# Transposes of the identity issued in TensorE's pauses at the four normalisations of a two-layer decoder trunk

## The reference

```
h = x
# layer 0
hn = rmsnorm(h, attn_norm[0]); h = h + hgrn2_mixer(hn, ...)      # gated recurrence, 8 heads, chunks of 64
hn = rmsnorm(h, ffn_norm[0]);  h = h + (silu(hn @ w_gate) * (hn @ w_up)) @ w_down     # 2816 hidden
k_band, v_band = shared_kv(h, kv_norm, kv_w, k_gain)             # its own rmsnorm of the same h
# layer 1
hn = rmsnorm(h, attn_norm[1]); h = h + swa_attention(hn, k_band, v_band, ...)
hn = rmsnorm(h, ffn_norm[1]);  h = h + moe_swiglu(hn, ...)       # top 2 of 8 experts, 3584 hidden
```

## Time and profile before

| What | Value |
|---|---|
| device time, three runs | 1426.94, 1434.97 and 1435.8 us, median 1434.97 |
| the profiled execution: device time | 1431.02 us |
| the profiled execution: span | 1428.3 us, so 2.7 us lie around it |
| mean granted TensorE clock | 0.977 of full speed |
| TensorE matmul busy | 1349.9 us, 95% of the span |
| VectorE, ScalarE, GpSimd busy | 334.2, 256.8 and 21.1 us |
| DMA | 442.49 MB, mean 310 GB/s |

### The profile page before, as it was taken

How to read it: one execution, slowest core, us unless ns; L and a number is a source line. 1 busy time by engine, 2 the same in 40 slices (tenths; PEclk the granted TensorE clock), 3 DMA queues, 4 the chain that set the end, 5 groups by cost and what they waited for, 6 DMA issues and landing times.

```text
span 1428.3 us, 32690 instructions
## 1 busy us (share of the span) xinstructions
PE 1349.9 (95%) x14751; PEld 795.1 (56%) x14751; DVE 334.2 (23%) x449; ACT 256.8 (18%) x367; POOL 21.1 (1%) x27
## 2 busy tenths in 40 slices
PE   6998899998889799999999999999999999999994
PEld 5997799987657533533543443453453453353352
DVE  5664455453676400000000000000000000000001
ACT  5453444433533100000000000000000000000000
POOL 0001000000000100000000000000000000000001
PEclk9999899999899799999999999999999999999997
DMA  9972455555521698699999999999999999999994
GB/s 324 327 236 73 131 178 184 200 181 182 183 73 60 263 354 307 259 419 343 389 419 391 378 417 405 377 414 414 361 412 419 358 410 420 368 407 420 379 388 169
DMA packets 123540, 442.49 MB, mean 310 GB/s; under 512 B 9028, under 2 KB 50196, under 8 KB 107028
## 3 DMA queue, kind: packets, MB, share of 16 engines
q1 hardware_dynamic: 117844, 425.24, 78.8%
q10 hardware_dynamic: 4416, 11.04, 2.1%
q0 software_dynamic: 1152, 4.19, 0.8%
HBM read 434.12 MB, written 12.08 MB: 312 GB/s over the span
## 4 chain that ended last, share of the span: by engine, by line
PE 93%; DVE 3%; DMA 1%; ACT 1%; issue 1%; POOL 0%; SPq 0%; POOLq 0%; DVEq 0%; ACTq 0%
PE bank L1481 41%; PE bank L1496 21%; PE bank L1167 8%; PE bank L1168 8%; PE bank L1169 8%; PE bank L1526 1%; PE bank L1186 1%; PE bank L1539 1%; PE bank L1376 1%; PE bank L1471 1%; PE bank L1268 1%; PE bank L1463 1%; PE bank L1332 0%; DMA raw<-in_hgrn_w_in 0%; DVE w_lo L742 0%
## 5 line engine op out<-in xcount | busy, mean ns | idle before, releaser
L1481 PE MATMUL bank<-raw,xT 128*32 128x512 f32 (+1 forms) x4608 | 442.1, 541 | 4.0 <-issue 3.3
L1481 PEld LDWEIGHTS bank<-raw,xT 128*32 128x32 f32 x4608 | 150.8, 110 | 284.7 <-issue 284.7
L1496 PE MATMUL bank<-dn,hidT 128*32 128x256 f32 x5376 | 296.5, 379 | 0.0
L1496 PEld LDWEIGHTS bank<-dn,hidT 128*32 128x32 f32 x5376 | 172.3, 110 | 116.1 <-issue 4.4
L742 DVE TENSOR_TENSOR w_lo<-raw,w_hi 128x2048 fp32r<-128x2048 f32 x63 | 144.1, 2291 | 123.8 <-ACT w_hi L509 123.6
L1142 DVE TENSOR_TENSOR e_hid<-e_silu,bank 128x512 f32<-128x512 f32 (+1 forms) x48 | 26.9, 617 | 532.1 <-PE bank L1481 532.1
L1481 PE MATMUL bank<-up_more,xT 128*32 128x384 f32 (+1 forms) x1536 | 150.2, 539 | 0.0
L1167 PE MATMUL bank<-ht_hi,w_hi 128*128 128x256 f32 x480 | 136.2, 284 | 0.0
L1168 PE MATMUL bank<-ht_lo,w_hi 128*128 128x256 f32 x480 | 135.7, 283 | 0.0
L1169 PE MATMUL bank<-ht_hi,w_lo 128*128 128x256 f32 x480 | 135.6, 282 | 0.0
L509 ACT ACTIVATE w_hi<-raw 128x2048 fp32r<-128x2048 f32 x63 | 120.1, 1908 | 60.2 <-PE bank L1169 59.5
(11 more groups left out here) (232 smaller groups left out, 807.4 us busy)
## 6 DMA issues: line engine op xcount, KB each, us to landing
dn<-in_moe_w_down SPq DMA_DIRECT2D x112, 1024.0 KB, 12.5
raw<-in_moe_w_gate SPq DMA_DIRECT2D x48, 1024.0 KB, 13.5
raw<-in_moe_w_up SPq DMA_DIRECT2D x48, 1024.0 KB, 12.1
raw<-in_moe_w_gate SPq DMA_DIRECT2D x48, 768.0 KB, 9.2
raw<-in_moe_w_up SPq DMA_DIRECT2D x48, 768.0 KB, 6.3
raw<-in_hgrn_w_in SPq DMA_DIRECT2D x16, 1024.0 KB, 11.3
up_more<-in_moe_w_gate SPq DMA_DIRECT2D x16, 1024.0 KB, 21.7
up_more<-in_moe_w_up SPq DMA_DIRECT2D x16, 1024.0 KB, 12.3
```

What stands on the lines that cost most here:

```text
L1481: ins = nc.tensor.matmul(out_banks[j][GTOK * c:GTOK * c + GTOK, 0:w], xT[:, kt, GTOK * g:GTOK * g + GTOK], chunk[:, w * b:w * b + w], star ...
L1496: ins = nc.tensor.matmul(banks[6 + j // 2][GTOK * c:GTOK * c + GTOK, 256 * (j % 2):256 * (j % 2) + 256], tok, dn[:, i % DN_RING, D * half ...
```

## The change

A helper `keep_busy(n, bank)` issues n transposes of the 128 by 128 identity, with the identity also as the operand that does the turning, into a bank that nobody reads. It is called ahead of the first quarter of each normalisation, and at the first three also between the second and the third quarter. These transposes wait on no semaphore and signal none. The counts are 8 and 16 at the first normalisation, 32 and 14 at the second, 50 and 16 at the third, and 38 at the fourth: 174 in all.

```diff
+            def keep_busy(n, bank):
+
+                for i in range(n):
+                    nc.tensor.transpose(bank[:, P * (i % 4):P * (i % 4) + P], ident, ident)
+
-            def turn_norm(i):
-
+            def turn_norm(i, bank, before, between):
+
+                keep_busy(before, bank)
                 for u in range(4):
+                    if u == 2:
+                        keep_busy(between, bank)
                     pe.wait_ge(xs_ready, 2 * (i - 1) + 1 + u // 2)
                     turn_rows(lambda t: xs[:, t, :], [u])
@@
-            turn_norm(1)
+            turn_norm(1, banks[5], 8, 16)
@@
-            turn_norm(2)
+            turn_norm(2, banks[5], 32, 14)
@@
-            turn_norm(3)
+            turn_norm(3, banks[1], 50, 16)
@@
             since = tp[0]
+            keep_busy(38, banks[0])
             for u in range(4 + 1):
                 if u < 4:
                     pe.wait_ge(hn_ready, 1 + u // 2)
                     turn_rows(lambda t: xs[:, t, :], [u])
```

## The result

| | before | after |
|---|---|---|
| device time, median of 6 runs each | 1433.3 us (1425.64 to 1435.8) | 1421.38 us (1417.76 to 1422.35) |
| ratio, 95% interval | | 0.9925 (0.9895 to 0.9954) |
| span of the profiled execution | 1428.3 us | 1420.1 us |
| mean granted clock | 0.977 | 0.983 |

The change gained 0.75%, some 11 us (4 to 15 us by the interval). The runs of before differ by how long the clock was at half: at a mean granted clock of 0.974 to 0.975 they take some 1434 us, at 0.979 some 1426, and a median of a few moves between the two.

The account below looks back on a forecast made before the run. TensorE was taken to bound the kernel, busy 95% of the span, its expert block only moving. Gains of 5.8 us less 1.6 given back make 4.2, so 1430.8 us against the median 1434.97; range 1425 to 1438.

Parts of the forecast that it names:

- The clock part: Ahead of the experts: fillers keep TensorE's granted clock at full through the normalisations, 4.2 us gained after what is given back.
- first: 1.5: First normalisation: the clock rises by 17 us instead of 20.4; gain 1.5 us, bounds 0 (even 0.2 lost) and 1.6.
- second: 1.6: Second normalisation: products run at full clock from their first one on; gain 1.6 us.
- given back at 130: -0.8: Around 129.8 us the clock still falls; work moves up, the rise stays, so half of the 1.5 us shift is lost.
- third: 1.0: Third normalisation: last quarter's transposes and the products behind run at full clock; gain 1.0 us, bounds 0 and 1.0.
- fourth: 1.7: Fourth normalisation: router records and the quarter after the first four run at full clock; gain 1.7 us.
- given back: -0.8: Between router and first expert product the clock still falls; 0.8 us of the shift lost, bounds 0 and 2.5.
- The stretch at 405.6: From 405.6 to 409.5 us, 16 transposes of xs against the identity held the clock at 1.00; evidence for holding.
- the gather: From 491.6 us, 16 matmuls moving zeros and ones left the clock at 0.50; evidence against identity transposes holding it.
- The first (identity transposes don't hold the clock): At the normalisations the clock falls as before; loss 2.2 us, 1433.2, or 1437.2 against the median; chance 0.17.
- the second (filler at half clock and late): Filler overruns the pauses at the second to fourth normalisation; 11.7 us late, 1442.7 or 1446.7 against the median; chance 0.06.
- Half of it: Held at second and fourth normalisation, not raised at first, fallen again at third between quarters; 2.5 us, 1432.5; chance 0.27.

Follow-up runs that it names:

- e1_pad92: The kernel before with 92 already met waits (46 instructions) at the start of TensorE's stream and no filler; 1426.8 us, ratio 0.9952 (0.9929 to 0.9974).
- e8_overfill: The changed kernel with twice the transposes ahead of the second, third and fourth normalisation (64, 100 and 76); 1424.5 us, one run.
- e11_more_fill_less16: The changed kernel with fillers also in the other pauses, less 16 transposes of that fuller version; 1413.8 us, ratio 0.9878 (0.9856 to 0.9900).
- e5_first_only: The kernel before with only the fillers of the first normalisation (8 and 16 transposes); 1426.7 us, ratio 0.9966 (0.9945 to 0.9988).

## Why the prediction was wrong, point by point

**The step that failed** is this sentence on what bounds the kernel: "The change touches nothing there; whatever it gains or loses ahead of the experts only moves that block". It touched the loop's place. The loop became 4.7 us faster at its back edges in the profile, and the place alone, with no filler, makes 0.9952 (0.9929 to 0.9974), 6.9 us with 3.7 to 10 us as bounds, by these middle values more than half of the whole. What the 2 us between 4.7 and 6.9 are is open; the interval takes in 4.7. The trace of before showed the cost: seven "issue" waits at the loop's first product, which the prediction put at nothing by not naming them. I had named the test for it (the stretch behind the first expert product taking another time), not the case.

**The clock part** was right in kind and about in size. The first expert product of the changed kernel is 5.3 us before that of e1_pad92 (505.54 and 500.28), which has its loop's speed and no filler; by the changed kernel's second profile (502.21) it is 3.3 us. I had forecast 4.2. In time it is not settled: 1421.4 or 1422.2 against 1426.8 is 5 us, but the ratios to the runs of before beside them, 0.9925 and 0.9948 against 0.9952, make 4 and 0.6 us, and all three intervals overlap. Stage by stage, as starts in e1_pad92 and in the changed kernel, good to 1 to 1.5 us each (the changed kernel's two profiles differ by as much in a stage):

| to the start of | e1_pad92 | after | gain in the stage | forecast |
|---|---|---|---|---|
| the turn of the recurrence's output | 126.46 | 124.88 | 1.6 | first: 1.5 |
| the first key and value product | 367.27 | 364.06 | 1.6 | second: 1.6, given back at 130: -0.8 |
| the first query by key product | 411.08 | 406.32 | 1.6 | third: 1.0 (0.4 of it in the row above) |
| the first router product | 485.19 | 480.63 | -0.2 | |
| the small matmuls of the routing | 493.33 | 488.06 | 0.7 | fourth: 1.7 |
| the first expert product | 505.54 | 500.28 | 0.0 | given back: -0.8 |

- **Held or not.** Held at all three in this profile, and raised at the first. The stretch at 405.6 was the right guide, and the gather the wrong one: in the changed kernel the clock rose at 499.2, with the gather only, before the first expert product at 500.28. At the third it is on the edge, as feared: of the five profiles with at least the change's fillers there, it fell for 3.4 us in three: in the changed kernel's second one (364.5 to 367.9), in e8_overfill and in e11_more_fill_less16.
- **First.** The rise came at 14.55 by the clock's records, not just "by 17". The gain of 1.6 meets the forecast in part by luck: the bound of 1.6, just under which I took 1.5, didn't bind. It took the end of the second chunk's w_lo at 22.8 as fixed (24.5 less 22.8 is also 1.7, not 1.6); in the changed kernel it ended at 22.13, and TensorE began that chunk at 22.63 without a wait, 1.3 us before e1_pad92 (23.92). Against before's own profile the stage is 2.7 us shorter (127.59 and 124.88).
- **Second.** From the turn of the recurrence's output to the first transpose of the second normalisation e1_pad92 took 34.80 us and the changed kernel 35.04, from there to the first transpose of the third 199.05 and 197.54: 1.5 us, the forecast's 1.6.
- **Fourth.** 0.7 for 1.7. The kernel before happened to have 6.8 us at half there, e1_pad92 3.4. Against before's own profile the stage gained 1.8 (from 9.19 to 7.43), as worked out; the term was sized from one execution's falls.
- **Given back.** 0.8 were forecast at 130. From the turn of the recurrence's output to the second normalisation the changed kernel took 0.2 us more than e1_pad92 in one profile and 1.2 in the other, e5_first_only 0.4: between nothing and the forecast, within the scatter. 0.0 over gather and wait as a whole. What I didn't name is the attention. Before was at half there for 3.4 us in its profile, the changed kernel and e1_pad92 for 13.6. From the first query by key product to the router this costs the changed kernel 2.9 us against before (71.4 and 74.3 us), and without it the two profiles would differ by some 5 us at the first expert product instead of 2.0. The profiled execution of before (granted clock 0.977, 1431.02 us) lies between the two ends of its runs.
- **The rivals.** The first (identity transposes don't hold the clock) and the second (filler at half clock and late) didn't occur; e8_overfill made the filler late by its count, and the real transposes started 2.3, 3.7 and 3.1 us late. Of "Half of it" one condition, the fall at the third between the quarters, came true in three of the five profiles, the other, no rise at the first, in none.
- **The range.** Its lower end was the clock part in full, less scatter. A case in which the rest of the kernel changes speed wasn't in it.

What stays open: why the packet ahead of the next item starts before the branch at places 0 to 92 and behind it at 108 and 124, where in its packet the loop's start and end lie, and what the loop's own setting does. The kernel writes the loop with `hint_back_edge=True` in both versions, and no run was made without it. The runs show the cost as a function of the place, and the traces that it is a wait for a packet of code, not why that packet is asked for when it is. The Trainium skill (Runtime: NRT & Kernel Launch, Instruction fetch mechanics) says that code is refilled in blocks of 256 instructions and that a taken branch out of the blocks at hand waits for a fetch. The 12 packets an item and the return of the stall at 256 agree with the blocks, and the 3 us from branch to packet at 108 and 124 with the wait. At 46 to 92 the runs differ from it: the packet starts 2 to 3.5 us ahead of the branch, and the branch costs nothing.

## What to carry to other kernels

Before a change adds or removes instructions ahead of a long loop, look at the idle "issue" time at the loop's back edge, and test the place by itself, with satisfied waits at the start of the stream: here it was worth -7 to +49 us, more than any edit of the work. Filling TensorE's pauses with transposes into a bank that nobody reads kept the clock at full, with these counts, at the second and fourth normalisation in every profile and at the third in two of five, and cost nothing where they ended before the release. Filling the other pauses as well was worth another 8 us (1422.2 to 1413.8). Then measure the place again, because each filler moves the loop. And take more than one profile: the two of the changed kernel differ by 1.9 us ahead of the loop.

## What the runs showed of the hardware that I had not expected

- A loop of 2957 TensorE instructions costs 0, 0.15 to 0.7 or over 4 us at a back edge (over 6 with the clock's fall behind it), by its place modulo 256 instructions: 0 and 256 ahead give items of 113.2 and 113.3 us, 46, 48, 76 and 92 give 112.52, 108 and 124 give 119.2 and more.
- What it waits for is a 16 KB packet of code: the next item's first instruction comes 1.4 to 1.7 us after the packet's end where TensorE stalls.
- Transposes alone raise the granted clock from half to full: with nothing but 8 of the identity and 8 of xs between, 8 took 1.97 us and the next 16 took 1.91. 50 of the identity by itself, 5.62 us of them, held it at 1.00.
- A gather with a moving matrix of zeros and ones raises it too: at 499.2 in the changed kernel, though not in the profile of before.
- A wait that is already met costs TensorE 0.11 us an instruction, two waits in each.
